# A recurrent gate projected in two parts, its bulk between the first query and the second merge

## What is computed

```python
h = rmsnorm(x, g_mix); proj = h @ w_in
xr, gr, qa, kva, qm, gates = jnp.split(proj, offsets, axis=-1)
xc, conv_last = causal_conv(xr, conv0, conv_w, conv_b)
y_lru, h_last = rglru(xc, h0, ...)          # recurrent, over time
y_lru = y_lru * jax.nn.gelu(gr)             # gr: the recurrent gate, 1024 features
...
merged = g_l * (y_lru @ w_o_lru) + g_a * (o_mla @ w_o_mla) + g_m * (o_mem @ w_o_mem)
x = x + merged @ w_out
x = x + peer(rmsnorm(x, g_ffn), ...)        # per token 8 heads x 16 of 16384 experts
return rmsnorm(x, g_final), ...
```

## Time and profile before

| | us |
|---|---|
| three runs | 4434.34, 4441.89 (median), 4444.01 |
| span of the profiled execution | 4435.2 |
| projection tiles 8 to 15 | 129.4 to 247.2 |
| first merge, out, query | 1070 to 1598.4 |
| second merge | 1598.4 to 2424 |
| out_b, second query | 2424 to 2785 |
| dense | 2785 to 3660 |
| tail, VectorE's rows | 3660 to 4435 |

### The profile page before, as it was taken

The page is one execution under the profiler, slowest core; times in us unless marked ns, Lnnn a source line. Parts: engine busy times, 40 slices in busy tenths (PEclk is TensorE's granted clock), DMA queues, the critical chain, the costliest instruction groups (busy, mean ns, idle before and its releaser), DMA issues.

```text
span 4435.2 us, 37982 instructions
## 1 busy us (share of the span) xinstructions
PE 3608.9 (81%) x13874; PEld 2263.2 (51%) x13874; DVE 2800.4 (63%) x3704; ACT 387.1 (9%) x897; POOL 1465.4 (33%) x1217
## 2 busy tenths in 40 slices
PE   9999999998999999999999999999999990000000
PEld 7888856645998575555555456444444440000000
DVE  5233324431000378887887668888885558999998
ACT  1012123321000100000000010000000001000000
POOL 0000100042000035454455444333322226777772
PEclk9999999999999999999999999999999995555555
DMA  4211361158666599999999989999999999999998
GB/s 183 76 68 67 118 222 43 43 185 293 244 240 247 207 390 399 412 418 400 384 406 421 418 358 370 412 405 417 419 401 423 423 423 374 395 409 410 410 410 368
DMA packets 224180, 1409.18 MB, mean 318 GB/s; under 512 B 33312, under 2 KB 44448, under 8 KB 60000
## 3 DMA queue, kind: packets, MB, share of 16 engines
q0 software_dynamic: 135632, 899.39, 50.0%
q1 hardware_dynamic: 75072, 471.89, 27.7%
q10 hardware_dynamic: 13296, 35.52, 2.1%
HBM read 1380.91 MB, written 25.75 MB: 317 GB/s over the span
## 4 chain that ended last, share of the span: by engine, by line
PE 69%; DMA 12%; DVE 6%; POOL 6%; issue 6%; ACT 1%; SPq 0%; DVEq 0%; POOLq 0%; ACTq 0%
PE psum L1217 20%; PE psum L1076 17%; PE psum L670 13%; DMA arena<-in_v,arena 10%; POOL arena L615 4%; PE psum L1196 4%; PE psum L1181 3%; POOL arena L645 2%; DVE arena L2111 2%; DVE psum L2275 2%; PE psum L1144 2%; PE psum L1124 1%; PE psum L743 1%; PE psum L753 1%; PE psum L904 1%
## 5 line engine op out<-in xcount | busy, mean ns | idle before, releaser
L1076 PE MATMUL psum<-arena 128*128 128x160 f32 (+1 forms) x5120 | 1174.1, 393 | 2.6 <-DMA arena<-in_w_merge 1.8
L2275 DVE SCALAR_TENSOR_TENSOR psum<-arena,psum 128x2048 f32<-128x2048 f32 x381 | 897.1, 2355 | 215.4 <-DMA arena<-in_v,arena 207.9
L1076 PEld LDWEIGHTS psum<-arena 128*128 128x128 f32 x5120 | 834.2, 190 | 342.1 <-DMA arena<-in_w_merge 2.0
L615 POOL DMA_INDIRECT arena<-in_v,arena x544 | 638.9, 1174 | 783.3 <-DVE psum L2275 365.0
L1217 PE MATMUL psum<-arena 128*128 128x512 f32 x2048 | 879.2, 592 | 0.6 <-ACT arena L1559 0.6
L615 POOL DMA_INDIRECT arena<-in_u,arena x288 | 462.2, 1605 | 1131.7 <-DVE arena L2028 504.0
L1217 PEld LDWEIGHTS psum<-arena 128*128 128x128 f32 x2048 | 389.1, 190 | 490.1 <-issue 490.1
L670 PE MATMUL psum<-arena 128*128 128x272 f32 x2432 | 565.0, 394 | 8.7 <-DMA arena<-in_w_proj 8.7
L670 PEld LDWEIGHTS psum<-arena 128*128 128x128 f32 x2432 | 461.9, 191 | 108.8 <-issue 14.8
L2072 DVE CUSTOM_DVE_ANT_1 arena<-arena 128x2048 f32<-128x2048 f32 x160 | 361.7, 2289 | 59.6 <-DMA arena<-in_u,arena 58.8
L2111 DVE SCALAR_TENSOR_TENSOR arena<-arena,pages 128x2048 f32<-128x2048 f32 x128 | 300.9, 2351 | 87.6 <-DMA arena<-in_v,arena 83.7
(11 more groups left out here) (312 smaller groups left out, 2559.4 us busy)
## 6 DMA issues: line engine op xcount, KB each, us to landing
arena<-in_w_merge SPq DMA_DIRECT2D x160, 1024.0 KB, 6.7
arena<-in_u_cols SPq DMA_DIRECT2D x128, 1024.0 KB, 9.5
arena<-in_w_out SPq DMA_DIRECT2D x32, 1024.0 KB, 6.3
arena<-in_w_query SPq DMA_DIRECT2D x32, 1024.0 KB, 6.9
arena<-in_w_proj SPq DMA_DIRECT2D x31, 1024.0 KB, 4.9
products<-arena ACTq DMA_DIRECT2D x32, 512.0 KB, 13.8
arena<-in_pool_keys SPq DMA_DIRECT2D x80, 160.0 KB
arena<-in_v,arena POOLq DMA_INDIRECT x544, 12.0
```

What stands on the lines that cost most here:

```text
L615: pool.indirect_dma_start(row, None, A[table], bass.IndirectOffsetOnAxis(ap=idx[:, r:r + 1], axis=0))\
L1076: last = mm(out, w[:, (off + k) * P:(off + k + 1) * P], src[:, k0 + k, lo:hi], start=(k == 0), stop=(k == n - 1))
L2275: V.scalar_tensor_tensor(a, four(row), atmp_b[:, t, r:r + 1], a if r else four(x1_b[:, t, :]), ALU.mult, ALU.add).then_inc(s("rows_used"), 1)
```

## The change

The gate `gr` is no longer projected for all 544 columns in front. Tiles 8 to 15 compute only pass A's 160 columns (one product of 160 columns in place of two of 272), and `keep_proj` stores those. `lru(c)` applies the gelu to these columns alone; for the other 384 it copies the recurrent output itself to where the gated one would stand.

A new stage `rnn_b` stands between `query_a` and `merge_b`: SyncE fetches the same 8 weight tiles again, TensorE projects pass B's 384 columns into two alternating banks, ScalarE squares them (the factor in the scale) and later takes the tanh, VectorE does the gelu's three multiplications and multiplies the copy in place (`rnn_out`). `merge(16)` waits for all eight (`rnn_used`, `lru_done`), as its first gate takes over the banks.

Around it: in front `project(16)` goes ahead of `lru_gates(0)` and of the wait for the memory norm, and that norm stands behind tile 15, not 11, on VectorE. In the new stage VectorE takes 22 rows (two or three per tile) and makes `pairs_a(3, 2)` and `pairs_a(3, 4)`, which stood in the second merge. The gelu of tile 3 moves from M = 24 to 23, and 263 rows are taken at the end of the merge, not 248. Ahead of the first `x1` of `out_b` stand 13 rows, not 10; 12 rows stand behind each of the first three; `u` of tile 2 is reached with 320 rows taken at the end of the norm (296 before). In the second query the rows per ranking change, 31 instead of 21 are taken of `u` of tile 2, and `pairs_b(2, 2)` is made in its last step. Two own-step counters are folded into other semaphores.

```diff
+STAGES: ("query_a", 16), ("rnn_b", 8), ("merge_b", 80)
+        def gr_bank(n):
+            return psum[:, 2 * proj_pair(n), 0:A_N]
+        def rnn_temp(c):
+            return hT[:, 3 * (c % 2):3 * (c % 2) + 3, A_LO:SEQ]
+        def rnn_in(c):
+            return three(psum[:, c % 2, 0:B_N])
...
+                    if 8 <= n < 16:
+                        last = mm(gr_bank(n), w[:, k * P:(k + 1) * P], hT[:, k, A_LO:T], start=(k == 0), stop=(k == KD - 1))
...
             for c in range(6):
+                if c == 0:
+                    project(16)
+                    pe.wait_ge(s("mem_inv"), 1)
                 lru_gates(c)
-                project(16 + 2 * c)
+                if c >= 1:
+                    project(16 + 2 * c)
                 project(17 + 2 * c)
...
+                if M == 16:
+                    pe.wait_ge(s("rnn_used"), 8)
                 prod(w, 0, hT, 0, KD, gate_bank(M, 0), s("w_used"))
...
+            for c in range(8):
+                w = weight(FIRST["rnn_b"] + c)
+                if c >= 2:
+                    pe.wait_ge(s("rnn_used"), c - 1)
+                for k in range(KD):
+                    last = mm(psum[:, c % 2, 0:B_N], w[:, k * P:(k + 1) * P], hT[:, k, 0:A_LO], start=(k == 0), stop=(k == KD - 1))
+                last.then_inc(s("w_used"), 1)
...
+            for c in range(8):
+                act.wait_ge(s("w_used"), FIRST["rnn_b"] + c + 1)
+                if c >= 2:
+                    act.wait_ge(s("lru_done"), NRNN + c - 1)
+                a_(rnn_temp(c), rnn_in(c), ACT.Square, scale=GELU_R).then_inc(s("rnn_squared"), 1)
+                act.wait_ge(s("lru_g"), NRNN + c + 1)
+                a_(rnn_temp(c), rnn_temp(c), ACT.Tanh, scale=GELU_S).then_inc(s("lru_gtanh"), 1)
...
+                do(V.tensor_copy(proj[:, GR + c, 0:A_LO], T1[:, 0:A_LO]))
...
-                if n == 11:
+                if n == 15:
                     norm("mem", psum[:, 6, 0:MEM], RU[:, 0:MEM], KD, D, lambda k: mn[:, k, :], "g_mem")
...
-            take(10)
+            def rnn_out(c):
+                g, h = rnn_temp(c), three(proj[:, GR + c, 0:A_LO])
+                dve.wait_ge(s("lru_gtanh"), NRNN + c + 1)
+                V.scalar_tensor_tensor(g, g, 1.0, rnn_in(c), ALU.add, ALU.mult).then_inc(s("rnn_used"), 1)
+                dve.wait_ge(s("rnn_used"), c + 1)
+                V.scalar_tensor_tensor(h, g, 0.5, h, ALU.mult, ALU.mult).then_inc(s("lru_done"), 1)
+            for c in range(8):
+                take(2)
+                if c in (2, 6):
+                    pairs_a(3, 2 if c == 2 else 4, 0)
+                dve.wait_ge(s("rnn_squared"), c + 1)
+                V.scalar_tensor_tensor(rnn_temp(c), rnn_temp(c), 1.0, rnn_in(c), ALU.add, ALU.mult).then_inc(s("lru_g"), 1)
+                take(0 if c in (2, 6) else 1)
+                rnn_out(c)
+            take(9)
             products_in(16)
-            take(1)
-            pairs_a(3, 2)
+            take(2)
...
-            take(10)
+            take(13)
             dve.wait_ge(s("x_tok_landed"), 32 + 48)
...
-                    take((12, 12, 6)[n])
+                    take(12)
...
-            take(3)
+            take(6)
```

More of the change, by code:

```diff
@@ L53 @@
 GELU_S = 0.7978845608028654
+GELU_R = GELU_A ** 0.5
 SLOT = 2048
@@ L174 @@
 U_TILES = 128
[L175 removed]
+STAGES = (("mla_v", 2), ("merge_a", 80), ("out_a", 16), ("query_a", 16), ("rnn_b", 8), ("merge_b", 80), ("out_b", 16), ("query_b", 16), ("dense", U_TILES))
 FIRST, WEIGHTS = {}, 0
@@ L2189, in _ @@
             dve.wait_ge(s("hf_done"), 3)
-            take(3)
+            take(6)
+            assert taken == first_row["u", 2]
             dve.wait_ge(s("hfT_stored"), 8 + 12)
```

84 lines of the change are left out of this document (45 added, 39 removed).

## The result

The changed kernel takes 4460.6 us (median of four runs, 4453.4 to 4462.7), the kernel before, on the same chip, 4443.0 (four runs, 4434.3 to 4445.9). The ratio is 1.0043, with a 95% interval of 1.0031 to 1.0055. The forecast was 4460, slower. The profiled executions say how the sum came about.

The account below looks back on a forecast made before the run. Bound: TensorE's work and few waits up to 3660 us, then a 775 us tail of VectorE weighing gathered rows. Terms −82.9 + 82.5 + 14.4 + 4 + 8.5 − 8 = +18.5 us, put on the median 4441.9: 4460, range 4437 to 4477.

Parts of the forecast that it names:

- (1): In front, eight projection tiles shrink from two halves of 272 columns to 160: −82.9 us, lru(0) losing nothing.
- (2): Everything between the front and the new stage runs as before, 83 us sooner; no cost of its own.
- (3): New stage between first query and second merge, 8 tiles of 32 passes at 384 columns: +82.5 us.
- (4): TensorE waits for VectorE at the new stage's tile 4 (3.2) and before merge 16 (11.2): +14.4 us.
- (5): Passes run slower behind the two new idle stretches of TensorE in the new stage: +4 us, bounds 2.6 and 5.
- (6): ScalarE's alternating squares and tanhs in the new stage: only one table load of 1.28 us, under a row.
- (7): TensorE's wait for x1 in out_b grows from 8.7 to 17 us, by three more rows and lag: +8.5 us.
- (8): Dense product's end to first gather from products: GpSimd stops earlier, so the last store lands sooner: −8 us, bounds −10 and 0.
- The sign that I gave: Ahead of the first gather from products, GpSimd would be idle 30 us or more.

Follow-up runs that it names:

- the front alone: Kernel before with only the eight front gate tiles cut to 160 columns, the new stage left out: 4353.1 us against 4438.5, ratio 0.9804.
- less fetched: Changed kernel with the new stage's eight weight tiles loaded only in their first 128 of 2048 columns: 4455.3 us, ratio 1.0039 to the kernel before.
- both edits: Changed kernel with one pairs_a call moved behind the stage's nine rows and 6 instead of 13 rows ahead of the first x1: 4432.5 us, ratio 0.9983.
- pairs later: Changed kernel with one pairs_a call moved from the new stage's seventh tile to behind the nine rows: 4450.4 us, ratio 1.0030 to the kernel before.
- both edits with the stop at 102: Changed kernel, pairs_a moved, 6 rows ahead of x1, GpSimd's stop at row 102 instead of 100, gathers spread: ratio 0.9986 to the kernel before.
- 6 rows: Changed kernel with 6 instead of 13 rows ahead of the first x1 in out_b, a tanh later: 4441.3 us, ratio 1.0008 to the kernel before.

## Why the prediction was right, step by step

The sum to the dense product's end was +26.5 and came out at +20.4; the tail was −8 and came out at −4.0; together +18.5 against +16.4. The mechanism held: the work moved at its own price, and VectorE's lateness at two places made the kernel slower. That the total came so near is in part luck. The parts ahead of the tail were 6.1 too high, the tail 4.0 too low, and 2.0 of the 6.1 is the spread between two single traces. By the parts:

- **(1) The front:** −82.9 forecast, −82.7 in the rows above (`project(16)` starts at 164.55). `lru(0)` cost nothing. The run of the front alone gives −82.2 for the span.
- **(2) Between:** forecast nothing; the first query ended at 1513.68, 84.7 ahead of before. The 2.0 us beyond the front are within what that end varies from trace to trace (above); nothing here ties them to the change.
- **(3) The stage:** 82.5 forecast, 83.1 measured.
- **(4) The two stalls:** 3.2 and 11.2 forecast, 2.45 and 10.58 measured. The walk of VectorE's operations held to 1.4 us; the runs with a pairs call moved (3.9) and with less fetched (10.6 unchanged) show that VectorE's own work was the cause, and not rows or weights that land late.
- **(5) The clock:** +4 forecast, about 2.2 measured (the second merge took 827.9 in place of 825.7). This term was mis-sized because I charged both stalls. Behind 10.58 us idle the granted clock was 0.50, the 1.2 GHz level, for the first 4.2 us; behind 2.45 it stayed at 1.00:

```profile
1609.80:1614.00 4.20, 4.20 (x7) 2.38 (x8) 4.20 (x4) 0.00 (x0) 3.59 (x3) 0.50 1.03 394
1614.00:1618.00 4.00, 4.00 (x13) 2.25 (x13) 4.00 (x5) 0.00 (x0) 3.39 (x3) 0.95 0.94 346
...
1557.70:1562.00 4.30, 4.30 (x14) 2.58 (x15) 4.30 (x4) 0.00 (x0) 0.84 (x1) 1.00 0.40 166
```

- **(6) Table loads:** one of 1.28 us in the stage, as forecast.
- **(7) out_b:** +8.5 forecast, +7.1 measured, for reasons that partly cancel. VectorE came out of the last merge 12.9 us behind TensorE (2437.73 to the first row at 2450.66), where it had been 15.2: I had said the same or 1 more. And three more rows made the stretch 53.7 − 44.3 = 9.4 longer, not 7.5: I had priced them by two rows behind `x1`, 2.5 us apart, where the ten ahead of it took 4.4 each. It was this price that was wrong; why those two were quicker no run tests.
- **(8) The tail:** −8 forecast, −4.0 measured. This term was mis-sized because I misread its start: I took the dense product's end as 3660, a round bound of a window, and so saw 14 us up to the first gather. It ended at 3664.90, and the gap was 9.4. In the twelve traces the gap is never under 5.2, so no more than 4.2 was to be had; the changed kernel got 4.1 of it. The sign that I gave failed too, GpSimd idle for 30 us or more: it stood for 18.3, its last row 14.0 us ahead of the end. That cost no time, since 8.4 is enough (above), but it shows how a lead is lost. GpSimd's rows alone, in three windows, of the changed kernel and then of before (rows asked for are the count in brackets):

```profile
0.00:2505.10 2505.10, 474.62 (x280) 0.99 0.68 261
2505.10:2805.00 299.90, 117.21 (x72) 0.99 0.86 342
2805.00:3671.40 866.40, 237.24 (x199) 1.00 0.99 408
...
0.00:2484.40 2484.40, 435.37 (x262) 0.99 0.65 252
2484.40:2785.00 300.60, 140.48 (x81) 0.99 0.94 376
2785.00:3660.70 875.70, 256.17 (x207) 1.00 1.01 416
```

The changed kernel is 18 rows ahead when `x1` is stored and 9 ahead when the dense product starts, where I had counted 10 for VectorE: so far the forecast held. I made 35 us of these, with the price that a row and a pairs call have on VectorE; but it asks for the row before the stop 1166 us behind `x1` where before it was 1176, only 10 less. At 4.2 us a row (207 rows in 875.7 us before) 9 rows are 38 us, so some 28 were lost inside the dense product, where its DMA engines moved 408 GB/s in place of 416. Most of them went in two stretches of 100 us, the first and the fifth. These are GpSimd's two waits and then the windows (GpSimd's busy time and rows, clock, DMA share, GB/s) of the changed kernel and of before:

```profile
2699.64 0.94 POOL L629 DMA_INDIRECT arena<-in_u,arena  x1 [55.03 <-DVE arena L2070]
2833.99 2.30 POOL L629 DMA_INDIRECT arena<-in_u,arena  x1 [21.44 <-DVE arena L2070]
...
2805.00:2905.00 100.00, 24.99 (x20) 1.00 0.92 372
3205.00:3305.00 100.00, 23.41 (x20) 1.00 0.94 369
...
2785.00:2885.00 100.00, 34.49 (x23) 1.00 1.01 415
3185.00:3285.00 100.00, 33.85 (x25) 1.00 0.98 395
```

L2070 is the last operation of a pairs call, which writes the indices of the next 32 rows. GpSimd came to `u` of tile 2 and stood 55.0 us until the first call had been made, and then 21.4 us for the second, which the changed kernel makes in the last step of the query. The kernel before waits for no indices from the second query on. I had counted the rows and not the indices that they need; why the fifth stretch lost 5 rows stays open.

The Trainium skill, "DMA: Bandwidth & Descriptors", section "Where 436 GB/s comes from", would have the rows of the new stage land late at its 358 GB/s. The trace disagrees again: in the stage the DMA engines moved 352 GB/s and VectorE waited for no row, and in the dense product they move more than 358 for 100 us on end:

```profile
3505.00:3605.00 100.00, 100.00 (x234) 44.29 (x234) 57.67 (x27) 5.06 (x8) 22.46 (x25) 1.00 1.01 423
```

The Trainium skill's page "HBM Reference", section "Specifications (TRN2)", has a core that streams alone at about 425, and with that the trace agrees.

## What to carry to other kernels

Work that is moved costs what it cost; what decides is who has to be ready beside it at the new place. Here the engine beside TensorE had 8% more to do in the new stage than TensorE, so the stage was as long as that engine; count both sides of a new stage, and put a long call (12.5 us of pairs) where the engine is idle anyway, not where the other waits for it. And where an engine is late for a result that the busiest engine needs, count the items queued ahead of it at the price that they have there, 4.1 us a row on full DMA engines, and put them behind: this was worth 11 us in one kernel (10 rows to 6) and 13 in the other (13 to 6), by their traces.

A lead in a queue is only worth something if the items can be asked for (here their indices came late), and only up to the point where another term binds (here 8.4 us). Measure the gap that the lead should close from the event that ends, not from the bound of a window.

## What the runs showed of the hardware

- An idle stretch of 2.45 us left TensorE's granted clock at 1.00; 3.94 us did so in one trace (both edits) and not in two others, where it was 0.67 for the next 4 us (pairs later, and both edits with the stop at 102); 10.58 gave 0.50 for 4.2 us. Of eight traces with 2.4 to 2.5 us idle ahead of the fifth tile, seven had the next 128 passes in 41.52 us and one (6 rows) in 43.21. Behind the short waits ahead of the second query (1.2 to 1.35 us the last of them) the first 64 passes took 20.9 us in six traces and 22.4 to 22.6 in six, in one of the latter (6 rows) at a granted clock of 0.60 for 4 us. The same idle time doesn't always cost the same, and 1.5 to 1.7 us between two traces can be this alone.
- The last store of 512 KB was seen 9 to 11 us after the last product with rows of 1 MB in flight, and 5 to 6 when the rows had stopped 7 us or more before: never sooner than 13.6 us behind the request for the last row, and never sooner than 5.2 behind the product. Rows asked for in between gained what they cost the store.
- Single traces of kernels that are the same up to the first query's end differ there by 6 us and, with the old front, by 11. A few us between the spans of two single traces are no evidence by themselves; count between two points of the same trace.
